# The order of the query tiles in a sparse attention stage, turned round in both halves

## Chip, cores and metric

The kernel runs on one core of one Trainium2 chip. The metric is the device time of one execution in microseconds (us). Three runs of the kernel before gave 2013.47, 2013.79 and 2018.54 us, with a median of 2013.79 us.

## What is computed

Two transformer parts run one after the other on a sequence of 512 tokens of width 1024, in float32. The first is a layer with windowed attention, a gated convolution and a mixture of experts. The second has two layers: one with index-selected and forgetting attention and an MLP, and one with the sparse attention that this document is about, and an MLP. The sparse attention adds three branches for each of 16 heads in two groups of keys (g = 0 and 1), cut here to what matters:

```python
p_c = masked_softmax(s_c, cmp_end[None, :] <= t[:, None])      # 31 compressed keys
o_c = einsum('bghqn,bngd->bqghd', p_c, vc)
valid_s = tok_pos <= t                                          # selected blocks, causal
o_s = einsum('bghqk,bgqkd->bqghd', masked_softmax(s_s, valid_s), v_g)
valid_w = (pos >= 0) & (pos <= t) & (pos > t - WINDOW_2)        # window of 512, causal
o_w = einsum('bghqk,bkgd->bqghd', masked_softmax(s_w, valid_w), vw)
out = gb[..., 0:1] * o_c + gb[..., 1:2] * o_s + gb[..., 2:3] * o_w
```

With 512 tokens all 8 blocks are kept and the window reaches over the whole sequence, so both long branches are plain causal attention: the queries of tile t (128 tokens, t = 0 to 3) need (t + 1) x 128 keys. Tile 3 has four times the columns of tile 0.

## The kernel before

Each engine runs its own hand-written list of work, and the lists are tied by semaphores. TensorE (PE) does the products and the transposes, VectorE (DVE) and ScalarE (ACT) work on the results in PSUM and split operands into a high and a low float32r part, GpSimd (POOL) scales probabilities and makes low parts of weights, and SyncE (SP) issues the loads of weights into a ring of three slots.

The sparse attention is a software pipeline over 136 **items**, built once as the list `nsa` (L745 to L753). There are two halves (c = 0, 1: four of a group's eight heads each), in each half four query tiles t, and in each tile 17 items: 16 "pair" items (4 heads x 2 branches x 2 groups, each with n = (t + 1) x 128 key columns), and one "cmp" item for the compressed branch, always 256 columns wide. Every engine loops over the steps i and handles item i, or an item some steps back:

- PE, step i (L2119): the scores of item i into a PSUM bank (L2142, two matmuls of n columns; L2138 for cmp), the n/128 transposes of the probabilities of item i - 7 (L2153), and, where item i - 10 closes a group of four, the values of the four (L2112, 4 x n/128 x 2 instructions' worth of work, shown as 8, 16, 24 or 32 rows; L2102 for cmp). Scores of an item wait until the item that had its bank before is masked. Up to item 15 there are two banks (psS), afterwards four (psS, psA).
- DVE: masks item i and takes its minimum for the softmax (L3619), takes reciprocals (L3579), and copies the transposed probabilities of odd items from PSUM (L3603).
- ACT: the exponential of item i (L2181, `scr<-scr,stat`), and the copies of the even items' transposed probabilities (`big<-psT`). A closed tile's output is rounded by ACT (`nsa_out_hi`), and DVE makes its low part (`nsa_out_lo`).
- POOL: multiplies by reciprocal and gate (L1322; L1318 for cmp).

Other work is put between the items at fixed step numbers, which do not depend on the tile. At steps 3, 4, 12 and 13 PE makes the scores of the compressed keys (L2089), and at steps 5, 6, 7 and 9 it turns the queries of the second half (L1346). Both use the two psA banks in turn, so each waits for the one two before it to be copied out. ACT copies the queries one step later (two copies for each turn, `nsa_q<-psA`) and DVE takes their low part two steps later (two instructions):

```python
NSA_JOBS = (("cmp", 0), ("cmp", 1), ("query", 4), ("query", 5), ("query", 6), ("query", 7), ("cmp", 2), ("cmp", 3))
NSA_STEPS = (3, 4, 5, 6, 7, 9, 12, 13)
```

At items 82, 86, 90 and 94 (`PRESPLIT`) ACT and POOL split a quarter each of the first weights of the output projection (`no_part`, L1290 on POOL). When the scores of item 67 are done, SP issues the load of `no1` into the slot where the queries of the first half lay. After the last item the pipeline drains, and the output projection (L1482, `no_part`, `nsa_out_hi`, `nsa_out_lo`) waits for the output of all eight tiles. Each tile's values gather in one of two psO banks, by `bank`.

Of the kernel before, what the change touches and what calls it, by code (L numbers as in the profile page):

```python
# [13 lines left out]
P = 128  # L14
T = 512
NT = T // P
# [318 lines left out]
def build(nc, w, out):  # L335
    ctx = ExitStack()
    with ctx:
# [300 lines left out]
        for g in range(2):  # L638
            for t in range(NT):
                lo, hi = max(0, t - 1), min(NT - 1, t + 1)  # L640
                n = (hi - lo + 1) * P
# [26 lines left out]
        for kind in ("fox", "latent"):  # L668
            for hp in range(4):
                for t in range(NT):  # L670
                    for half in range(2):
                        pairs.append(dict(fox=kind == "fox", hp=hp, half=half, t=t, n=(t + 1) * P,
                                          bank=hp + 4 * (kind == "latent"), chunk=hp + 4 * (kind == "fox"),
# [70 lines left out]

        nsa = []  # L745
        for c in range(2):
            for t in range(NT):
                for j in range(4):
                    for branch in range(2):
                        for g in range(2):  # L750
                            nsa.append(dict(kind="pair", c=c, t=t, j=j, branch=branch, g=g, n=(t + 1) * P,
                                            head=8 * g + 4 * c + j, bank=NT * c + t, first=not j, closes=bool(branch and g)))
                nsa.append(dict(kind="cmp", c=c, t=t, g=1, n=2 * P, bank=NT * c + t, index=NT * c + t, closes=True))  # L753
        n_nsa = len(nsa)
        last_of = {it["bank"]: i for i, it in enumerate(nsa)}
        n_items = n_band + n_pairs
# [2908 lines left out]
```

How the kernel before makes its waits and increments, by code:

```python
        def product(eng, n, i=0):  # L934
            eng.wait_ge(proj_ready, i * 10 + (n + 1))
# [1 line left out]
        def copied(eng, n, i=0):  # L938
            eng.wait_ge(proj_evacuated[n % 2], i * 5 + (n // 2 + 1))
# [33 lines left out]
        def consumed(eng, l, i):  # L974
            kind, e, n = MLP_PIECES[i]
            if kind == "up":
                product(eng, job(f"mlp{l}", MLP_FIRST[kind, e] + n))
            elif e < LAST and n in KEPT:
                eng.wait_ge(down_product, len(KEPT) * (LAST * l + e) + KEPT.index(n) + 1)
            elif e < LAST:
                product(eng, job(f"mlp{l}", MLP_FIRST[kind, e] + 2 * SHARED.index(n) + 1))
            else:
                product(eng, job(f"mlp{l}", MLP_FIRST[kind, e] + NT * (n // 2 + 1) - 1))
# [64 lines left out]
        def spilled(eng):  # L1049
            eng.wait_ge(slots_ready, 2)
            return eng.value_load(spill_expert[0:1, 0:1], min_val=0, max_val=SPILL)
# [23 lines left out]
            def experts():  # L1077
# [1 line left out]
                def gate_up(n):  # L1079
                    if n >= UNITS:
                        sp.wait_ge(gu_ready, (n - UNITS) // 2 + 1)
                    e = PAIRS * (n % 2) + n // 2
                    load_gate_up(n % UNITS, slice(e, e + 1), gu_arrived[n % UNITS])
# [5 lines left out]
                    load_down(n % UNITS, slice(e, e + 1), dn_arrived[n % UNITS])  # L1089
                sp.wait_ge(y_zeroed, 16)
                sp.wait_ge(*held[gu_slot[0]])
# [1 line left out]
                product(sp, JOBS["mergea"] + KD - 1)  # L1094
                down(0)
                sp.wait_ge(*held[gu_slot[1]])
                gate_up(1)
```

## Time and profile before

| what | value |
|---|---|
| median of three runs | 2013.79 us |
| the profiled execution's own time | 2014.52 us |
| its span, first to last instruction | 2012.7 us |
| mean granted TensorE clock | 0.982 |
| busy over the span: PE, DVE, ACT, POOL | 94%, 50%, 41%, 28% |
| sparse attention: first scores | 1444.1 us |
| first instruction of the output projection | 1617.7 us |

The span is 1.8 us shorter than the profiled execution's own time, and that time is 0.7 us above the median. Times inside the span are counted from its first instruction. A PE instruction's duration includes its way through the array, so instructions that follow each other overlap, and "busy" overstates the work; the step from one start to the next is the better price.

### The profile page before, as it was taken

The page shows a single profiled execution, that of the slowest core. Times are in us where ns is not written, and L with a number is a line of the kernel's source. Part 1 is how long each engine was busy: PE and PEld are TensorE (multiplying, and loading weights), DVE is VectorE, ACT ScalarE, POOL GpSimd, SP SyncE. Part 2 cuts the span into 40 slices and gives each one's busy share as a digit, 9 for nine tenths or more (in the row PEclk, how much of TensorE's full clock was granted, in tenths as well). Part 3 has the DMA queues.
Part 4 walks back from the last instruction along what each step waited for, and adds up shares of the span by engine and source line. Part 5 has one row for each costly group of instructions (what it writes and reads, how often), then busy time and mean ns, then how long its engine had stood idle before and what let it go on. Part 6 is the DMA issues. An engine that isn't in the chain of part 4 may idle for free.

```text
span 2012.7 us, 28214 instructions
## 1 busy us (share of the span) xinstructions
PE 1883.7 (94%) x11022; PEld 1471.7 (73%) x11022; DVE 1012.7 (50%) x2027; ACT 815.8 (41%) x1507; POOL 559.2 (28%) x396
## 2 busy tenths in 40 slices
PE   7999999898888999988999999999899999999997
PEld 6878889832323893457888888888867798888886
DVE  2170442521113625863366676822566715676677
ACT  5123551311112413364554544343367626544542
POOL 2244331011110420154421123233146533113111
PEclk9999999999899999999999999999999999999999
DMA  6223303799999320201123223311103012223321
GB/s 234 85 84 123 129 1 147 274 375 419 421 420 346 133 103 0 84 1 43 43 97 113 84 84 126 136 57 43 42 2 85 2 43 84 84 84 126 126 84 42
DMA packets 86149, 252.10 MB, mean 125 GB/s; under 512 B 12132, under 2 KB 19492, under 8 KB 73728
## 3 DMA queue, kind: packets, MB, share of 16 engines
q1 hardware_dynamic: 80624, 237.83, 32.0%
q0 software_dynamic: 4592, 9.30, 1.3%
q10 hardware_dynamic: 800, 3.15, 0.4%
q8 instruction: 89, 1.46, 0.3%
q14 instruction: 44, 0.36, 0.1%
HBM read 241.89 MB, written 15.73 MB: 128 GB/s over the span
## 4 chain that ended last, share of the span: by engine, by line
PE 48%; DVE 4%; issue 2%; ACT 2%; POOL 0%; DVEq 0%; ACTq 0%
PE psA L1482 33%; PE psO L1647 2%; PE psT L1647 2%; PE psS L1647 2%; PE psO L2112 2%; PE psT L2153 1%; DVE x L2711 1%; PE psA L1598 1%; PE psS L2142 1%; PE psO L1546 1%; PE psT L1578 1%; ACT big L2181 1%; PE psA L2142 1%; DVE scr L3619 1%; PE psA L2022 1%
## 5 line engine op out<-in xcount | busy, mean ns | idle before, releaser
L1187 POOL TENSOR_TENSOR w_slot<-ring,w_slot 128x1024 fp32r<-128x1024 f32 (+2 forms) x80 | 208.4, 2620 | 550.8 <-ACT w_slot L2181 550.3
L1482 PE MATMUL psA<-hT_hi,w_slot 128*128 128x512 f32 x960 | 297.9, 389 | 0.0
L2181 ACT ACTIVATE w_slot<-ring 128x1024 fp32r<-128x1024 f32 (+2 forms) x178 | 191.9, 1088 | 176.9 <-PE psA L1482 76.9
L1482 PEld LDWEIGHTS psA<-hT_hi,w_slot 128*128 128x128 f32 x960 | 180.2, 188 | 37.5
L2711 DVE TENSOR_TENSOR x<-psA,x 128x512 f32<-128x512 f32 (+1 forms) x206 | 122.4, 623 | 147.1 <-PE psA L1482 142.5
L1482 PE MATMUL psA<-hT_lo,w_slot 128*128 128x512 f32 x480 | 186.7, 389 | 0.0
L2711 DVE TENSOR_TENSOR w_slot<-ring,w_slot 128x1024 fp32r<-128x1024 f32 x98 | 119.8, 1224 | 115.8 <-ACT w_slot L2181 115.8
L2181 ACT ACTIVATE big<-psA 128x512 f32<-128x512 f32 (+7 forms) x145 | 63.9, 465 | 255.5 <-PE psA L1482 140.1
L1482 PE MATMUL psA<-w_slot,hid_part 128*128 128x512 f32 x672 | 161.4, 389 | 0.0
L2181 ACT ACTIVATE scr<-scr,stat 128x384 f32<-128x384 f32 (+3 forms) x224 | 124.4, 556 | 68.0 <-DVE stat L3619 37.9
L1482 PEld LDWEIGHTS psA<-w_slot,hid_part 128*128 128x128 f32 x672 | 126.2, 188 | 26.1
L1187 POOL TENSOR_TENSOR ring_lo<-ring,early_hi 128x1024 fp32r<-128x1024 f32 x34 | 82.5, 2430 | 128.0 <-ACT early_hi L2181 128.0
L1322 POOL TENSOR_SCALAR scr<-scr,stat,big 128x128 f32<-128x128 f32 (+3 forms) x128 | 77.4, 616 | 108.5 <-DVE stat L3579 108.0
L1482 PEld LDWEIGHTS psA<-hT_lo,w_slot 128*128 128x128 f32 x480 | 90.1, 188 | 18.4
L2711 DVE TENSOR_TENSOR hid_part<-scr,hid_part 128x512 fp32r<-128x512 f32 x98 | 98.9, 1032 | 3.0 <-ACT hid_part L2181 1.8
L2181 ACT ACTIVATE hid_part<-scr 128x512 fp32r<-128x512 f32 x98 | 59.7, 625 | 98.3 <-DVE scr L2711 98.3
L1482 PE MATMUL psA<-w_slot,hT_hi 128*128 128x256 f32 (+2 forms) x512 | 93.9, 287 | 5.3 <-DVE tok L2715 2.7
L2711 DVE TENSOR_TENSOR big<-psA,small 128x512 f32<-128x512 f32 x32 | 20.6, 685 | 140.1 <-PE psA L1346 140.1
L1482 PE MATMUL psA<-hT_lo_early,early_hi 128*128 128x512 f32 x224 | 88.0, 393 | 0.0
L1840 PE MATMUL psS<-ring,big 128*64 128x512 f32 x192 | 74.9, 671 | 12.7 <-issue 12.7
L1482 PEld LDWEIGHTS psA<-w_slot,hT_hi 128*128 128x128 f32 x512 | 81.4, 197 | 5.9 <-issue 3.0
L2181 ACT ACTIVATE big<-psS 128x256 f32<-128x256 f32 (+1 forms) x20 | 7.3, 365 | 190.6 <-PE psS L1840 162.7
(440 smaller groups left out, 4473.5 us busy)
## 6 DMA issues: line engine op xcount, KB each, us to landing
ring<-in_mlp_w SPq DMA_DIRECT2D x32, 2048.0 KB, 8.1
ring<-in_w_in SPq DMA_DIRECT2D x8, 2048.0 KB, 8.0
ring<-in_w_gate_e SPq DMA_DIRECT2D x14, 1024.0 KB, 17.9
ring<-in_w_up_e SPq DMA_DIRECT2D x14, 1024.0 KB, 22.8
ring<-in_w_down_e SPq DMA_DIRECT2D x13, 1024.0 KB, 27.1
big<-in_w_down_e SPq DMA_DIRECT2D x12, 1024.0 KB, 28.2
ring<-in_ab_w_in SPq DMA_DIRECT2D x5, 2048.0 KB, 8.3
scr<-in_w_down_e SPq DMA_DIRECT2D x7, 1024.0 KB, 25.3
```

The source lines that it names most:

```text
L1187: nc.gpsimd.tensor_tensor(part(w_lo, c), raw_piece(c), part(w_hi, c).bitcast(F32), ALU.subtract)\
L1322: nc.gpsimd.tensor_scalar(at, at, fac[:, n_items + i:n_items + i + 1], gate3[:, it["t"], it["head"], 1 + it["branch"]:2 + it["branch"]], A ...
L1482: ins = pe.matmul(o, a, b, start=(at == 1), stop=(at == 3 * len(terms)))
L1546: ins = pe.matmul(o[HD * half:HD * (half + 1), t * P:(t + 1) * P], v[:, b, 2 * it["hp"] + half, :], pt[half][:, b * P:(b + 1) * P], start= ...
L1578: ins = pe.transpose(psT[k % 2][:, b * P:(b + 1) * P], pair_probs[k % PROBS][:, b * P:(b + 1) * P], ident)
L1598: ins = pe.matmul(out[f][:, some], a[:, k, 0:P], b[:, k, some], start=(k == 0 and a is wh and b is hT_hi), stop=(k == KD - 1 and a is wl))
L1647: ins = pe.matmul(KEPT_BANK[q][t][:, :], a[:, k, at], b[:, k, :], start=(not e and k == 0 and a is hi and b is wh), stop=(e == LAST - 1 an ...
L1840: ins = pe.matmul(psS[p][at:at + ROWS, :].rearrange("p (h n) -> p h n", h=2), xT[:, p, k, at:at + ROWS], gu[(2 * b + half) % UNITS][:, k], ...
L2112: ins = pe.matmul(o[HD * g:HD * (g + 1), at:at + P], v2[:, b, branch, g, 0:HD], pt[g][:, b * P:(b + 1) * P], start=(it["first"] and not br ...
L2142: ins = pe.matmul(o[:, 0:it["n"]], query(4 * it["c"] + it["j"], it["g"])[:, it["t"] * P:(it["t"] + 1) * P], nsa_k[:, it["branch"], it["g"] ...
L2181: return nc.scalar.activation(o, i, f, **kw)
L2711: return nc.vector.tensor_tensor(o, a, b, op)
```

## The change

The tiles of each half are taken in the order 3, 2, 1, 0, where they were taken 0, 1, 2, 3. `place` now numbers the PSUM bank, so that banks follow each other as before, while `t` still names the tile. Nothing is added or removed, and the fixed step numbers of the other work stay.

```diff
         for c in range(2):
-            for t in range(NT):
+            for place, t in enumerate((3, 2, 1, 0)):
                 for j in range(4):
                     for branch in range(2):
                         for g in range(2):
                             nsa.append(dict(kind="pair", c=c, t=t, j=j, branch=branch, g=g, n=(t + 1) * P,
-                                            head=8 * g + 4 * c + j, bank=NT * c + t, first=not j, closes=bool(branch and g)))
-                nsa.append(dict(kind="cmp", c=c, t=t, g=1, n=2 * P, bank=NT * c + t, index=NT * c + t, closes=True))
+                                            head=8 * g + 4 * c + j, bank=NT * c + place, first=not j, closes=bool(branch and g)))
+                nsa.append(dict(kind="cmp", c=c, t=t, g=1, n=2 * P, bank=NT * c + place, index=NT * c + t, closes=True))
```

On PE, at the start of the stage (`psS` holds scores, `psT` turned probabilities, `nsa_q_90` the queries of the first half, `par` and `const` constants and parameters), before:

```order
L2142 MATMUL psS<-nsa_k,nsa_q_90 128x128 x6
L2089 MATMUL psA<-nsa_q_90,big 32x512 x4
L2142 MATMUL psS<-nsa_k,nsa_q_90 128x128 x2
L2089 MATMUL psA<-nsa_q_90,big 32x512 x4
L2142 MATMUL psS<-nsa_k,nsa_q_90 128x128 x2
L1346 MATMUL psA<-const,tok 128x128 x4
L2142 MATMUL psS<-nsa_k,nsa_q_90 128x128 x2
L1346 MATMUL psA<-const,tok 128x128 x4
```

and now:

```order
L2142 MATMUL psS<-nsa_k,nsa_q_90 128x512 x6
L2089 MATMUL psA<-nsa_q_90,big 32x512 x4
L2142 MATMUL psS<-nsa_k,nsa_q_90 128x512 x2
L2089 MATMUL psA<-nsa_q_90,big 32x512 x4
L2142 MATMUL psS<-nsa_k,nsa_q_90 128x512 x2
L1346 MATMUL psA<-const,tok 128x128 x4
L2142 MATMUL psS<-nsa_k,nsa_q_90 128x512 x2
L1346 MATMUL psA<-const,tok 128x128 x4
```

The fixed work keeps its places, and the scores between its pieces are four times as wide.

On PE, the last rows of the stage, from the last scores (L2138) to the first row of the output projection, before:

```order
L2138 MATMUL psA<-const,big 128x128 x2
L2153 MATMUL psT<-const,scr 128x128 x8
L2112 MATMUL psO<-big 64x128 x16
L2153 MATMUL psT<-const,scr 128x128 x16
L2112 MATMUL psO<-big 64x128 x16
L2153 MATMUL psT<-const,scr 128x128 x6
L2112 MATMUL psO<-big 64x128 x16
L2102 MATMUL psO<-big 64x128 x8
L1482 MATMUL psA<-no_part_72,nsa_out_hi_93 128x256
```

and now:

```order
L2138 MATMUL psA<-const,big 128x128 x2
L2153 MATMUL psT<-const,scr 128x128 x2
L2112 MATMUL psO<-big 64x128 x4
L2153 MATMUL psT<-const,scr 128x128 x4
L2112 MATMUL psO<-big 64x128 x4
L2153 MATMUL psT<-const,scr 128x128 x3
L2112 MATMUL psO<-big 64x128 x4
L2102 MATMUL psO<-big 64x128 x8
L1482 MATMUL psA<-no_part_72,nsa_out_hi_93 128x256
```

What is left to do after the last scores shrinks to a quarter in the transposes and values of pair items and stays in those of the cmp item. (One row of this kind stands as two instructions in the trace, for float32.)

## Rows read from the trace of the kernel before

**Rows 1.** Busy time by stretch: each tile's scores, then the drain; header first.

```profile
core 0: us, PE busy (x) PEld busy (x) DVE busy (x) ACT busy (x) POOL busy (x), PEclk, DMA share, GB/s
1444.00:1470.60 26.60, 17.84 (x112) 10.53 (x100) 13.31 (x59) 14.63 (x50) 5.28 (x12) 0.74 0.00 1
1470.60:1484.60 14.00, 13.05 (x117) 10.37 (x118) 10.84 (x52) 10.75 (x39) 8.40 (x17) 1.00 0.01 2
1484.60:1503.30 18.70, 17.81 (x168) 14.83 (x167) 14.15 (x56) 13.24 (x42) 9.90 (x17) 1.00 0.01 1
1503.30:1527.80 24.50, 23.08 (x215) 18.39 (x214) 17.64 (x57) 17.17 (x45) 13.88 (x19) 1.00 0.01 1
1527.80:1545.20 17.40, 16.82 (x194) 14.56 (x192) 11.16 (x57) 10.86 (x42) 8.09 (x16) 1.00 0.92 242
1545.20:1561.40 16.20, 13.20 (x119) 10.42 (x119) 11.78 (x58) 13.60 (x49) 14.09 (x22) 1.00 0.01 3
1561.40:1580.10 18.70, 17.81 (x168) 14.77 (x167) 14.15 (x56) 13.04 (x42) 10.18 (x17) 1.00 0.01 2
1580.10:1604.00 23.90, 22.51 (x210) 17.82 (x209) 17.28 (x56) 16.60 (x44) 13.32 (x19) 1.00 0.00 1
1604.00:1617.70 13.70, 11.00 (x146) 9.43 (x144) 7.14 (x18) 6.11 (x13) 4.28 (x6) 1.00 0.01 2
```

**Rows 2.** Chain that ended last, by time: start us, us taken, what.

```profile
1446.08 1.07 PE psA L2089 x8
...
1471.22 0.59 PE psO L2112 x8
...
1595.47 1.02 PE psO L2102 x16
...
1597.15 0.44 PE psT L2153 x4
1597.59 0.46 PE psA L2142 x2
...
1600.30 1.90 PE psO L2112 x32
```

**Rows 3.** Timeline of PE, first stretch: start, us, instruction, [idle before <-releaser].

```profile
1453.24 1.12 PE L1346 MATMUL psA<-const,tok 128*128 128x128 f32 x4 [2.13 <-DVE nsa_q L2711]
...
1458.17 1.12 PE L1346 MATMUL psA<-const,tok 128*128 128x128 f32 x4 [2.70 <-DVE nsa_q L2711]
...
1464.67 1.55 PE L2089 MATMUL psA<-nsa_q,big 128*32 128x512 f32 x8
```

**Rows 4.** Groups by form, ACT, 1444 to 1618 us: count, busy us, mean ns, idle before.

```profile
L2181 ACT ACTIVATE scr<-scr,stat 128x512 f32<-128x512 f32 x32 | 22.9, 718 | 15.6 <-DVE stat L3619 15.4
...
L2181 ACT ACTIVATE big<-psT 128x512 f32<-128x512 f32 x16 | 9.4, 588 | 4.6 <-PE psT L2153 4.6
...
L2181 ACT ACTIVATE nsa_q<-psA 64x512 fp32r<-64x512 f32 x8 | 4.7, 586 | 0.1
```

**Rows 5.** Groups by form, DVE, the same stretch.

```profile
L3603 DVE COPY big<-psT 128x512 f32<-128x512 f32 x16 | 10.9, 683 | 9.7 <-PE psT L2153 9.5
...
L3619 DVE CUSTOM_DVE_ANT_0 scr<-psS,const 128x512 f32<-128x512 f32 x16 | 10.9, 679 | 0.0
...
L2711 DVE TENSOR_TENSOR nsa_q<-psA,nsa_q 64x512 fp32r<-64x512 f32 x8 | 5.5, 688 | 2.3 <-ACT nsa_q L2181 2.2
```

**Rows 6.** Busy time, part of the first stretch (PEclk is the column after POOL).

```profile
1451.00:1465.00 14.00, 8.46 (x39) 5.53 (x42) 7.85 (x23) 7.04 (x21) 1.97 (x5) 0.54 0.00 0
```

**Rows 7.** Groups by form, the weight splits inside the stage, ACT and POOL.

```profile
L2181 ACT ACTIVATE no_part<-ring 128x512 fp32r<-128x512 f32 x4 | 2.5, 614 | 0.0
...
L1290 POOL TENSOR_TENSOR no_part<-ring,no_part 128x512 fp32r<-128x512 f32 x4 | 5.3, 1328 | 0.0
```

**Rows 8.** Timeline of the drain, all engines: last scores, last output, projection.

```profile
1604.03 0.38 PE L2138 MATMUL psA<-const,big 128*128 128x128 f32 x2
...
1616.32 0.60 ACT L2181 ACTIVATE nsa_out_hi<-psO 128x512 fp32r<-128x512 f32 x1 [2.94 <-PE psO L2102]
...
1617.74 0.48 PE L1482 MATMUL psA<-no_part,nsa_out_hi 128*128 128x256 f32 x2 [1.47 <-ACT nsa_out_hi L2181]
```

**Rows 9.** Timeline of SP's queue: the load of the last projection slot.

```profile
1527.67 1.27 SPq L1170 DMA_DIRECT2D ring<-in_c_w_out  x2
```

## The prediction

> **What bounds the kernel now.** I read the busy time cut at the first scores of each tile first, because the change moves whole tiles and nothing else [rows 1]. The nine stretches are eight tiles and the drain, 173.7 us together. PE has granted clock 1.00 in eight of them and 0.74 in the first. Then I took from the chain of waits what PE's pieces cost when they follow each other [rows 2]: scores of a tile-3 item 0.46 us, its four transposes 0.44 us, so 0.11 or so per 128 columns for either; values of a group of four 1.90 us for tile 3 (32 instructions) and 0.59 for tile 0 (8), so about 1.46 and 1.02 for tiles 2 and 1 (24 and 16); values of the cmp item 1.02; one product with the compressed keys 1.07.
>
> With these prices I add up PE's work in each stretch. A stretch holds the scores of its own 17 items, but the transposes of items 7 back and the values of items 10 back, so it depends on the tile ahead of it too: of that one, 6 pair items and the cmp item are transposed and 3 groups and the cmp item get their values. Written as "tile after tile", with length, work and what is unfilled (the difference):
>
> - tile 0, first: 26.6, work 10.0 (6.0 of it the fixed work: 4 products and 4 query turns of 0.44), unfilled 16.6
> - 1 after 0: 14.0, 11.0, unfilled 3.0
> - 2 after 1: 18.7, 16.1, unfilled 2.6
> - 3 after 2: 24.5, 21.5, unfilled 3.0
> - 0 after 3: 17.4, 13.6, unfilled 3.8
> - 1 after 0, with the weight splits: 16.2, 11.0, unfilled 5.2
> - 2 after 1: 18.7, 16.1, unfilled 2.6; 3 after 2: 23.9, 21.5, unfilled 2.4
> - drain of tile 3: 13.7, 9.6, unfilled 4.1
>
> Work is 130.4 and unfilled time 43.3 us. So the stage is PE's with small losses everywhere but at its start, and the start is where a tile of little PE work meets fixed work that waits for ACT and DVE. PE stands 2.13 us and 2.70 us there for DVE's low parts of the queries [rows 3], and during it the granted clock is 0.54, near the lower level of 1.2 GHz [rows 6].
>
> **The change, part by part.** PE's work is the same in sum: by the same prices it comes out as 19.9 (tile 3 first), 20.2, 14.9, 9.6 (tiles 2, 1, 0), 17.6 (3 after 0), 20.2, 14.9, 9.6 and a drain of 3.7, 130.6 in all. Only the unfilled time can move.
>
> *First stretch.* I follow the waits with tile-3 durations: mask 0.68 (the next can start after 0.60), exponential 0.72 (next after 0.70), copies from psT 0.59 on ACT and 0.68 on DVE, two query copies 1.2 on ACT and two low parts 1.4 on DVE [rows 4, 5].
> (1) Start to the first query wait's end: the first two masks and DVE's small copies between them take ACT's second exponential to 3.2 us after the start; then ACT does three exponentials (2.1), the two copies of products with an exponential between (1.9), waits about 0.4 for mask 5, and does one exponential more (0.7) and the query copies (1.2), and DVE its low parts (1.4): about 11 us. Before it was 9.2, from 1444.0 to 1453.24 [rows 1, 3].
> (2) To the second query wait's end: query turn 0.44, scores 0.46, transposes with their latency 0.6, ACT copy 0.6, exponential 0.7, query copies 1.2, low parts 1.4: 5.4 us, before 4.9.
> (3) To the last product with the compressed keys: turn and scores 0.9, transposes and scores 0.9, transposes 0.6, DVE copy and mask 1.4, exponential 0.7, query copies 1.2, low parts 1.4: 7.1 us, before 6.5, at the low clock [rows 3].
> (4) To the first scores of the next tile: product 1.07, a wait for a mask 0.3, three steps of 0.9, values 1.9, the cmp step 0.7: 6.7 us, before 5.9.
> Together 30.2 us for 19.9 of work: 10.3 unfilled, a gain of 6.3 against 16.6. Its bounds: all waits overlapping with PE's work except the two query waits (7 unfilled) and all waits as now (16.6).
>
> *The seven tile changes.* Before, five of them without splits or tile 3 ahead left 2.4 to 3.0 unfilled, 2.7 on average, tile 0 after 3 left 3.8, and the splits added 2.2 to their stretch [rows 1]. I take 2.7 for each and 1.2 for the splits: these now fall on the last items of tile 3 and on tile 2, where ACT has more slack under PE (four splits are 2.5 us of ACT and 5.3 of POOL [rows 7]). That is 20.1 against 22.6, a gain of 2.5. Bounds: 2.4 each and no cost of splits (16.8), or 3.8 each and 2.2 (28.8).
>
> *The drain.* The cmp item's own latency (masks, exponential, POOL, transposes, copy, values, rounding) doesn't shrink with the tile, and the last output still goes over ACT and DVE before the projection, 1.4 us [rows 8]. PE's work falls from 9.6 to 3.7, but less of the latency lies under it: 4.6 unfilled against 4.1, a loss of 0.5. Bounds 4.1 and 5.5.
>
> *What hides the rest.* The load of `no1` starts when half of the scores are done, 83.6 us into the stage [rows 9]; by the lengths above that is now 83 us, and the slot is wanted only in the second half of the projection. No wait is added, and no queue is passed: SP and POOL keep their lists.
>
> Sum: 6.3 + 2.5 - 0.5 = 8.3. I take off 0.8 because PE still stands twice for some 3 us in the first stretch, and the clock may fall for a short while there. Gain 7.5 against the profiled execution's own 2014.5 us: 2007.0. That execution is 0.7 above the median of the runs, so against the median it is 2006.3 us.
>
> **A rule that speaks against it.** In the fourth stretch, where a third of PE's work is transposes (6.6 of 21.5 us), the granted clock is 1.00 throughout [rows 1]. The Trainium skill ("TensorE: Matmul & The Clock Gate", "PE-mode transpose") says that a transpose does not count as activity for the clock as a matmul does. Here the trace does not bear that out as a danger in a dense stretch, but the first stretch is not dense; what a low clock there would cost is the third rival.
>
> **The rivals.**
> - *The start only swaps its waits* (0.26). ACT and DVE carry the same 10 us of query copies among exponentials and masks 0.3 to 0.4 us longer each, 17 of either. If PE also waits for masks in between, through the two psS banks, the first stretch is 34 us instead of 30.2. For it: each engine runs strictly in order and [rows 3] show the waits in series. Against it: DVE is busy only 13.3 of 26.6 us there. Gain 3.5: 2010.3 us.
> - *The later stretches fill better too* (0.15). Bursts of values run ahead of narrower tiles, and everything after a wide tile finds its probabilities ready: unfilled 2.4 each and no cost of splits, gain 11: 2003 us. Against it is tile 0 after 3, with 3.8.
> - *The clock stays low from the first query wait on* (0.07, ends slower). In the first stretch PE would pay a further 10 us for the pieces on the path in (2) to (4), and if the low clock goes on into tile 2, up to 20 more. It decides from the point where 13.5 us of PE's path run at 1.2 GHz: 7.5 to gain and 6 to be slower by 0.3%. For it: 14 us of the first stretch ran so before [rows 6]. Against it: tile 3 gives PE twice the work there. Price 15: 2021 us.
> - That the change does not do what it says is left out: the two places shown in the order of the instructions say that it does.
>
> By the rule of the skill the clock would be at its lower level in the first stretch, and the time that of the third rival or a little below it.
>
> **How the numbers follow.** The forecast has 0.52. 0.3% of the median is 6.0 us, about what a measurement of this kernel can tell from no change. The forecast's own range, a gain of 5 to 10 us, lies mostly over that: 0.44 of it faster, 0.08 the same. The second rival is all faster (0.15), the first nearly all the same (0.25, 0.01 faster), the third 0.05 slower and 0.02 the same. That makes 0.60, 0.35 and 0.05. For 8 in 10 the range must hold the forecast, the first rival and most of the second, 2002.5 to 2012.5; the bounds together (3 us slower to 15 faster) are wider than that, and leave out what would need all terms at one end.
>
> **What would show it.** First scores of the second tile 30 us after the stage's first, against 26.5, with two waits for `nsa_q` of some 3 us left; clock 1.00 or nearly in that stretch; 12 to 13 us for the stretches of tile 0 and 20 to 21 for tile 3 after 0; 8 us between last scores and projection, against 13.7; everything outside the stage unchanged. It is wrong if the first stretch is over 33 us, if a clock of 0.5 shows for more than a few us, or if tile changes leave over 3.5 us each.

## The result, and the profile after

The changed kernel took 2022.12 us, median of ten runs (2019.91 to 2023.85); the kernel before took 2014.26 us beside it (2013.13 to 2018.54). The ratio is 1.0037, with a 95% interval of 1.0029 to 1.0045. The forecast was 2006.3 us in a range up to 2012.5, so the change costs 8 us where it should have given 8. The profiled execution took 2023.29 us, 1.2 above the median.

Busy time by stretch, the changed kernel, with the columns of [rows 1]: tiles 3, 2, 1, 0 of the first half, the same of the second, and the drain.

```profile
1443.90:1482.00 38.10, 25.86 (x163) 16.31 (x154) 21.76 (x59) 21.09 (x49) 9.14 (x12) 0.91 0.00 1
1482.00:1506.50 24.50, 23.36 (x225) 20.13 (x226) 14.32 (x51) 13.77 (x39) 11.29 (x17) 0.93 0.01 2
1506.50:1524.00 17.50, 17.01 (x182) 14.29 (x180) 12.68 (x57) 12.21 (x43) 9.19 (x16) 1.00 0.01 1
1524.00:1538.80 14.80, 13.12 (x133) 10.59 (x131) 10.28 (x57) 10.31 (x45) 8.51 (x18) 1.00 0.00 1
1538.80:1559.20 20.40, 19.49 (x155) 14.43 (x155) 15.68 (x56) 14.39 (x42) 10.67 (x17) 1.00 0.83 208
1559.20:1584.80 25.60, 22.12 (x227) 18.58 (x226) 16.34 (x57) 17.63 (x49) 17.44 (x22) 1.00 0.01 2
1584.80:1602.30 17.50, 16.99 (x182) 14.28 (x180) 12.69 (x57) 12.19 (x43) 9.53 (x17) 1.00 0.01 1
1602.30:1616.60 14.30, 12.71 (x130) 10.40 (x129) 9.78 (x53) 9.80 (x42) 8.31 (x17) 1.00 0.01 2
1616.60:1625.00 8.40, 5.26 (x53) 3.32 (x51) 4.83 (x21) 4.28 (x16) 3.25 (x7) 1.00 0.01 2
```

The stage takes 181.1 us, against 173.7 [rows 1]. With the prediction's PE work for each stretch, the unfilled times are 18.2, 4.3, 2.6, 5.2, 2.8, 5.4, 2.6, 4.7 and 4.7, together 50.5 against 43.3 before. The first stretch alone is 38.1 where 30.2 was forecast. So that stretch holds half of the 15.8 us between forecast and result. Its granted clock is 0.91, against 0.74 before, so on the whole it was less slowed by the clock than the stretch before the change; but the prediction had priced (2) to (4) at full clock and taken off only 0.8, and what the low clock cost is worked out below.

Busy time after the stage, to the end of the program, the changed kernel and then the kernel before:

```profile
1625.00:2021.50 396.50, 382.61 (x1916) 325.91 (x1916) 246.95 (x308) 180.22 (x239) 104.28 (x41) 0.99 0.24 85
```

```profile
1617.70:2012.70 395.00, 381.14 (x1916) 324.56 (x1916) 246.75 (x308) 180.23 (x239) 104.26 (x41) 0.99 0.24 86
```

Same work, 1.5 us more. It lies where the projection ends and the first products of the MLP begin; in the changed kernel that piece has granted clock 0.91, before 1.00:

```profile
1672.00:1690.00 18.00, 14.74 (x106) 13.62 (x105) 8.12 (x15) 8.75 (x14) 7.74 (x4) 0.91 0.12 41
```

```profile
1664.70:1682.70 18.00, 14.75 (x118) 13.62 (x118) 8.11 (x15) 8.91 (x16) 7.77 (x4) 1.00 0.14 40
```

The stage's 7.4 us and these 1.5 are, but for rounding, the 8.8 us between the two spans.

PE's timeline at the end of the first stretch of the changed kernel (it answers to [rows 3]):

```profile
1455.67 1.11 PE L1346 MATMUL psA<-const,tok 128*128 128x128 f32 x4 [2.55 <-DVE nsa_q L2711]
...
1459.00 0.60 PE L2153 MATMUL psT<-const,scr 128*128 128x128 f32 x4
1462.61 1.12 PE L1346 MATMUL psA<-const,tok 128*128 128x128 f32 x4 [3.02 <-DVE nsa_q L2711]
...
1465.89 0.60 PE L2153 MATMUL psT<-const,scr 128*128 128x128 f32 x4
...
1471.45 1.07 PE L2089 MATMUL psA<-nsa_q,big 128*32 128x512 f32 x8 [0.19 <-DVE nsa_q L2711]
1472.82 0.73 PE L2142 MATMUL psS<-nsa_k,nsa_q 128*128 128x512 f32 x2 [0.30 <-DVE stat L3619]
1473.38 0.60 PE L2153 MATMUL psT<-const,scr 128*128 128x128 f32 x4
1473.91 1.97 PE L2112 MATMUL psO<-big 128*64 128x128 f32 x32
1475.81 0.73 PE L2142 MATMUL psS<-nsa_k,nsa_q 128*128 128x512 f32 x2
1476.38 0.60 PE L2153 MATMUL psT<-const,scr 128*128 128x128 f32 x4
1478.36 0.73 PE L2142 MATMUL psS<-nsa_k,nsa_q 128*128 128x512 f32 x2 [1.39 <-DVE stat L3619]
...
1479.79 0.41 PE L2138 MATMUL psS<-const,big 128*128 128x128 f32 x2 [0.25 <-ACT big L2181]
...
1482.02 0.61 PE L2142 MATMUL psS<-nsa_k,nsa_q 128*128 128x384 f32 x2 [1.39 <-DVE stat L3619]
```

and DVE's over the same time:

```profile
1472.76 0.67 DVE L3619 CUSTOM_DVE_ANT_0 scr<-psS,const 128x512 f32<-128x512 f32 x1
...
1477.01 0.69 DVE L3603 COPY big<-psT 128x512 f32<-128x512 f32 x1 [3.58 <-PE psT L2153]
1477.62 0.68 DVE L3619 CUSTOM_DVE_ANT_0 scr<-psS,const 128x512 f32<-128x512 f32 x1
```

The two views have to be laid over each other. The scores of item 13 start at 1472.82, and with 0.73 us for their two instructions they are done by 1473.6. DVE has been idle since 1473.4, but it doesn't mask them: its list has a copy of item 7's transposes ahead of mask 13. PE makes those transposes one step later (1476.38), behind item 14's scores, and both stand behind 1.9 us of values. So DVE idles 3.58 us, mask 13 runs at 1477.62, and only then may PE write item 15's scores into the bank: 1478.36, after 1.39 us of waiting. **PE and DVE wait for each other in a ring.** PE turns item i - 7 at step i, but DVE (odd items) and ACT (even items) copy item i - 6 at step i, *before* the mask or exponential of item i. In each of the prediction's steps (2) to (4) this ring lies across the path, and the copy, the mask and the values in it are 0.69, 0.68 and 1.9 us for tile 3, where tile 0 had 0.29, 0.28 and 0.59.

### The profile page after: what moved, and what is told of

The parts are those of the page before. It is cut to its first block, busy times and chain, and to the rows that moved or that the text cites. A ratio compares the mean times of both kernels' runs of the same rounds, so it can differ in the third digit from the quotient of the medians.

```text
span 2021.5 us, 28214 instructions
## 1 busy us (share of the span) xinstructions
PE 1888.1 (93%) x11022; PEld 1474.4 (73%) x11022; DVE 1014.1 (50%) x2027; ACT 815.6 (40%) x1507; POOL 559.3 (28%) x396
## 4 chain that ended last, share of the span: by engine, by line
PE 48%; DVE 4%; issue 2%; ACT 2%; POOL 0%; DVEq 0%; ACTq 0%
PE psA L1482 33%; PE psO L1647 2%; PE psT L1647 2%; PE psS L1647 2%; PE psO L2112 2%; PE psT L2153 2%; DVE x L2711 1%; PE psA L1598 1%; PE psS L2142 1%; PE psO L1546 1%; PE psT L1578 1%; DVE scr L3619 1%; PE psA L2142 1%; PE psA L2022 1%; ACT big L2181 0%
## 5 line engine op out<-in xcount | busy, mean ns | idle before, releaser
L1322 POOL TENSOR_SCALAR scr<-scr,stat,big 128x512 f32<-128x512 f32 (+3 forms) x128 | 77.5, 616 | 119.8 <-DVE stat L3579 119.7
L1482 PEld LDWEIGHTS psA<-hT_lo,w_slot 128*128 128x128 f32 x480 | 90.1, 188 | 18.7
## 6 DMA issues: line engine op xcount, KB each, us to landing
ring<-in_w_up_e SPq DMA_DIRECT2D x14, 1024.0 KB, 20.3
```

What stands on the lines that cost most here:

```text
L1322: nc.gpsimd.tensor_scalar(at, at, fac[:, n_items + i:n_items + i + 1], gate3[:, it["t"], it["head"], 1 + it["branch"]:2 + it["branch"]], A ...
L1482: ins = pe.matmul(o, a, b, start=(at == 1), stop=(at == 3 * len(terms)))
```

## The experiments

Each run was timed in five rounds; ratios are to the kernel before on the same chip. Lengths of stretches are from first scores to first scores, in each profiled execution.

### Which resource holds the start: banks or query copies

Two simple theories came first. Theory A: the first 16 items have only two psS banks, and scores wait for masks through them. Theory B: the four query turns, close together at steps 5, 6, 7 and 9, pile up copies on ACT and DVE. What theory A blames is undone by a third bank, in both kernels:

```diff
-            return psS[i % 2] if i < MORE_BANKS else (psS + psA)[i % 4]
+            return (psS[1], psO[1], psS[0])[i % 3] if i < MORE_BANKS else (psS + psA)[i % 4]
```

> The changed order with a third PSUM bank for the scores of items 0 to 15 (one psO bank, which is idle until item 30's step). Theory A (two score banks are too few for tile 3: a score waits for the mask of two items before, which waits behind DVE's copy of a transposed item, five waits, 5.1 us in all): first stretch 38.1 us falls to 33 to 34, time 2017 to 2018 us. Rival B (the fixed work is a series chain over ACT and DVE of 5.9 us of waits for query low parts, and a third bank only lets PE arrive there earlier): first stretch 37 to 38.5, time 2021 to 2023.

Measured: 2025.53 us, ratio 1.0054 (1.0040 to 1.0067). The first stretch stays 38.1 us, and the second takes 25.3, 0.8 more than in the changed kernel. Where PE waited in the first, for the changed kernel:

```profile
PE psA L1346 <- DVE nsa_q L2711: 5.6, 2, 3.0
PE psS L2142 <- DVE stat L3619: 5.1, 5, 1.5
```

and with the third bank (us in all, times, longest):

```profile
PE psA L1346 <- DVE nsa_q L2711: 5.6, 2, 3.0
PE psA L2089 <- DVE nsa_q L2711: 2.0, 1, 2.0
PE psS L2138 <- ACT big L2181: 1.9, 1, 1.9
PE psS L2142 <- DVE stat L3619: 1.4, 1, 1.4
```

3.7 us of waits for masks are gone, and 3.4 us come back as waits for DVE's low parts and ACT's copies. Theory A, which expected 33 to 34 us for this stretch, falls: the banks are where the wait shows, not what makes it.

> The kernel before, with the same third bank. Theory A: with tile 0 a mask takes 0.28 us instead of 0.69 and a copy 0.29 instead of 0.69, so the bank binds less than half as much: 1 to 2.5 us faster than before, 2012 to 2013 us. Rival B: no difference over 0.5 us, 2014.

Measured on the kernel before: 2016.27 us, ratio 1.0006 (0.9997 to 1.0015), first stretch 26.8. No difference in the time that can be told from zero, as rival B had it. In its profiled execution the waits for masks fell from 2.4 to 0.6 us, but the second stretch took 15.3 us instead of 14.0, with a second piece at the lower clock (1471.1 to 1474.5 us).

Theory B was tried by spreading the fixed steps:

```diff
-NSA_STEPS = (3, 4, 5, 6, 7, 9, 12, 13)
+NSA_STEPS = (1, 2, 3, 4, 7, 8, 12, 13)
```

> The changed order with the fixed work spread: steps 1, 2, 3, 4, 7, 8, 12, 13 in place of 3, 4, 5, 6, 7, 9, 12, 13, so that a query turn stands four steps behind the one whose bank it takes, not two. Theory B (the first stretch is a series chain: turn, ACT copies, DVE low parts, next turn, with tile 3's masks, exponentials and copies between its links): the waits of 2.55 and 3.02 us before the query turns go, first stretch 38.1 to 32 to 34, time 2016 to 2018 us. Rival (the sum of the work of ACT and DVE per step is the limit, wherever the links stand): 37 to 38 and 2021 to 2023.

Measured: 2023.55 us, ratio 1.0038 (1.0026 to 1.0050), first stretch 37.7. PE's waits there:

```profile
PE psS L2142 <- DVE stat L3619: 7.6, 6, 2.7
PE psA L1346 <- DVE nsa_q L2711: 1.4, 2, 1.0
```

The query waits shrink from 5.6 to 1.4 us, the mask waits grow from 5.1 to 7.6, and PE stands 1.8 us before a product with the compressed keys for a reason that the profile doesn't name. What was gained on one link was lost on others: theory B, which expected 32 to 34 us, falls as well, in its simple form.

> The kernel before with the same spread steps. Theory B: the waits of 2.13 and 2.70 us go, and with them the low clock; first stretch 26.5 to 22 to 23, time 2010 to 2011 us, 3 to 4 us under the kernel before. Rival: 26 and 2014.

Measured on the kernel before: 2016.54 us, ratio 1.0006 (0.9997 to 1.0015), first stretch 26.7. The low clock did not go, as theory B had hoped: PE ran at it from 1455.5 to 1465.7 us and again from 1469.1 to 1475.9, and the second stretch took 15.5 us instead of 14.0.

### Which half, which place

```diff
-            for place, t in enumerate((3, 2, 1, 0)):
+            for place, t in enumerate(((0, 3, 2, 1), (3, 2, 1, 0))[c]):
```

> Tiles 0, 3, 2, 1 in the first half and 3, 2, 1, 0 in the second: only the first tile is put back beside the fixed work. Theory that the whole loss is the first stretch (38.1 against 26.5 us, less than the 9.9 us of more PE work there explains): first stretch 26.5 again, and the time 2014 to 2016 us. Rival (descending order loses in each stretch that follows a wider tile, and at tile 0): 2018 to 2020 us.

Measured: 2020.75 us, ratio 1.0029 (1.0016 to 1.0041). With tile 0 first the first stretch is 26.6 us again, and tile 3 after 0 takes 19.7, tile 2 22.2, tile 1 19.2 (with the work that a tile 3 leaves behind it), and the second half is 21.8, 25.6, 17.4, 14.3 and a drain of 9.8: 176.6 us in all, 2.9 above the kernel before. So 4.5 of the stage's 7.4 us hang on the wide tile at the start, and the rest doesn't. Two stretches of this one run have the same PE work, tile 2 after tile 3, without and with the weight splits:

```profile
1491.60:1513.80 22.20, 21.60 (x229) 18.75 (x227) 15.82 (x57) 14.56 (x42) 10.26 (x16) 1.00 0.01 2
1554.80:1580.40 25.60, 22.11 (x227) 18.57 (x226) 16.33 (x57) 17.64 (x49) 17.46 (x22) 1.00 0.01 2
```

The splits cost 3.4 us in this place; the prediction had 1.2. In the changed kernel's stretch with splits PE and its weight loads waited so, and in the stretch without (of this run) the second of the two waits was 0.9 us, once:

```profile
PE psT L2153 <- ACT big L2181: 3.5, 3, 1.3
...
PEld psT L2153 <- POOL scr L1322: 4.6, 4, 1.6
```

A split of 1.27 us on POOL stands in its list between scalings of 0.66 us, and one of 0.61 us on ACT ahead of the copies of transposes. Both kinds of wait grow beside them; which of the two engines sets the 3.4 us was not tried apart.

```diff
+            for place, t in enumerate(((0, 1, 2, 3), (3, 2, 1, 0))[c]):
```

> First half as before (0, 1, 2, 3), second half turned round (3, 2, 1, 0). By unfilled PE time: start 16.6, then 3.0, 2.6, 3.0 as before, then tile 3 after 3 about 2, tile 2 with the splits 5.4, tile 1 2.5, tile 0 4.8 and the drain 4.6 as in the changed kernel: 44.5 against 43.3, so 1 us slower than before, 2014 to 2016.5 us. If turning round the second half alone were a gain (its stretches with the drain are 86.2 us in the changed kernel and 89.9 before), 2010 to 2011 us.

Measured: 2018.63 us, ratio 1.0020 (1.0011 to 1.0029). Stretches 26.6, 14.0, 18.7, 49.8 (the two tiles 3 side by side), 25.6, 17.4, 14.3 and a drain of 9.4: 175.8 us, 2.1 above the kernel before. The order turned in the second half alone loses too.

```diff
+            for place, t in enumerate(((3, 2, 1, 0), (0, 1, 2, 3))[c]):
```

> Only the first half turned round (3, 2, 1, 0), the second as before. The unfilled times of the changed kernel's first half (18.2, 4.3, 2.5, 5.2), about 4 for tile 0 after tile 0, and those of the kernel before for the rest (5.2, 2.6, 2.4, 4.1) make 48.5 against 43.3: 2019.5 us. If the loss were all in the second half, 2014 us.

Measured: 2021.78 us, ratio 1.0026 (1.0014 to 1.0037). Stretches 38.1, 24.5, 17.4, 26.8 (two tiles 0), 16.2, 18.7, 23.9 and a drain of 13.7: 179.4 us. So the new order of the first half alone makes 5.7 of the stage's 7.4 us of loss.

### The lag between the lists

Theory S: what makes tile 3 dear at the start is the ring, PE's transposes of item i - 7 against copies of item i - 6 on the other engines. Theory L: it is the plain latency of mask, exponential and scaling, and a shorter lag makes PE wait for that. The two are told apart by taking PE's turns and values one item earlier (6 and 9 back), in the three lists of the stage:

```diff
-AHEAD, MORE_BANKS, PRESPLIT = 2, 16, (82, 86, 90, 94)
+AHEAD, NSA_AHEAD, MORE_BANKS, PRESPLIT = 2, 1, 16, (82, 86, 90, 94)
...
-                    k = i - TURN_LAG - AHEAD
+                    k = i - TURN_LAG - NSA_AHEAD
...
-                    k = i - VALUE_LAG - AHEAD
+                    k = i - VALUE_LAG - NSA_AHEAD
```

> The changed order, with transposes and values one step earlier in PE's list (items 6 and 9 back instead of 7 and 10). Theory L (what is unfilled at tile 0 and 1 behind wider tiles is the latency from scores over mask, exponential, reciprocal and POOL to the transpose, which must fit into 7 steps of PE): with 6 steps every stretch of tile 0 and 1 gets 1 to 3 us longer, time 2027 to 2032. Theory S (DVE's copy of item i - 6 waits in front of mask i for the transposes that PE makes one step later, 41 us of waits in all, and that delays everything): the waits of DVE L3603 halve, time 2015 to 2019.

Measured: 2015.60 us, ratio 1.0003 (0.9994 to 1.0012). Stretches 32.9, 22.4, 17.9, 13.6, 24.0, 23.6, 17.9, 12.6 and a drain of 7.7: 172.7 us where the changed kernel takes 181.1. DVE's waits for transposes over the whole stage, changed kernel, then this one:

```profile
DVE big L3603 <- PE psT L2153: 52.2, 36, 4.3
```

```profile
DVE big L3603 <- PE psT L2153: 37.5, 33, 2.7
```

They fall by 28%, not by the half that was expected, and the longest from 4.3 to 2.7 us. The time lies where theory S had it (2015 to 2019), and L, with 2027 or more, falls.

> The kernel before with the shorter lag (6 and 9) everywhere. Theory S with the loop's price by width: copy and mask are 0.57 us with tile 0 and 1.38 with tile 3, so the first stretch gains 1 to 2 us of 26.5, the others together 0 to 3: 2010.5 to 2013.5 us, and the order 0 to 3 stays ahead of 3 to 0 (2015.6 with the same lag). Rival (with the shorter lag the order no longer matters, or the turned order profits alone): 2014.5 to 2016.

The same edit on the kernel before: 2013.64 us, ratio 0.9995 (0.9986 to 1.0004), stage 172.5 us. The lag is worth 8.4 us of the stage with the wide tiles first and 1.2 with the narrow first, and with lag 6 the two orders take the same (172.7 and 172.5). So the stage's loss hangs on the two together: the wide-first order loses only with the long lag. The 8.4 us are not all waits, though. With lag 6 the wide-first kernel has none of its three pieces at the lower clock left, while the narrow-first one keeps its long one (13.6 us, 13.7 before).

Is it the start alone? Only PE's items up to step 16 take the short lag, step 17 turns nothing, and everything behind is as in the changed kernel:

```diff
-                    k = i - TURN_LAG - AHEAD
+                    k = i - TURN_LAG - 1 if i < MORE_BANKS + 1 else i - TURN_LAG - AHEAD if i > MORE_BANKS + 1 else -1
...
-                    k = i - VALUE_LAG - AHEAD
+                    k = i - VALUE_LAG - 1 if i < MORE_BANKS + 1 else i - VALUE_LAG - AHEAD if i > MORE_BANKS + 1 else -1
```

> The changed order with the shorter lag (6 and 9) for PE's steps 0 to 16 only, and 7 and 10 from step 18 on. If the loop of DVE's copy, mask and PE's next step is what made the first stretch 38.1 us and not 30.2, this takes it to 33 as the shorter lag everywhere did (32.9), and leaves the other stretches as in the changed kernel: 2016.5 to 2018. If the gain of the shorter lag was spread or came from the granted clock by luck, 2020 to 2022.

Measured: 2016.12 us, ratio 1.0005 (0.9996 to 1.0014). Its first two stretches:

```profile
1444.00:1476.90 32.90, 25.03 (x197) 15.94 (x190) 22.93 (x61) 22.61 (x53) 10.76 (x14) 1.00 0.00 1
1476.90:1497.30 20.40, 19.27 (x192) 16.56 (x191) 13.14 (x47) 12.09 (x36) 9.62 (x16) 1.00 0.01 2
```

Together they take 53.3 us, where the changed kernel takes 62.6 for the same work (one group of values and four transposes, 2.3 us, lie in the first stretch here and in the second there). The prediction had 53.1 for the two. DVE's waits for transposes from 1438 to 1483 us, in this kernel, then in the changed one:

```profile
DVE big L3603 <- PE psT L2153: 6.1, 4, 2.0
```

```profile
DVE big L3603 <- PE psT L2153: 11.1, 4, 4.0
```

The second row is the waits for items 1, 3, 7 and 9 (4.02, 1.81, 3.58 and 1.69 us). With the short lag these are 1.64, 0, 1.88 and 0.59, together 4.1 instead of 11.1; the fourth wait of the first row, 2.0 us, is for item 11, later than anything in the second. PE's wait before item 15's scores is 0.48 us instead of 1.39:

```profile
1472.56 0.73 PE L2142 MATMUL psS<-nsa_k,nsa_q 128*128 128x512 f32 x2 [0.48 <-DVE stat L3619]
```

**About half of these 9.3 us is the clock.** Behind each of its two long query waits the changed kernel's PE does a turn, scores, transposes and scores again before the transposes on which DVE's copy waits. From 1455.67 to 1459.00 and from 1462.61 to 1465.89 that takes 3.33 and 3.28 us at the lower clock. With the short lag the same four pieces run at full clock and take 1.86 us both times:

```profile
1455.73 0.66 PE L1346 MATMUL psA<-const,tok 128*128 128x128 f32 x4 [2.11 <-DVE nsa_q L2711]
...
1457.59 0.60 PE L2153 MATMUL psT<-const,scr 128*128 128x128 f32 x4
1460.29 0.66 PE L1346 MATMUL psA<-const,tok 128*128 128x128 f32 x4 [2.11 <-DVE nsa_q L2711]
...
1462.15 0.60 PE L2153 MATMUL psT<-const,scr 128*128 128x128 f32 x4
```

That is 2.9 us in the first stretch. In the second, the changed kernel has a third such piece; from the 4.00 us that PE is busy there at granted clock 0.57 (shown below) it costs an estimated 1.7 us, and the same work took 2.3 us less in the run that starts with tile 0. The other 4 to 5 us are waits at full clock, those for items 7 and 9 and behind them. So the ring costs by its waits, and as much again by the clock that falls behind them; that the ring's waits are what makes it fall is argued from the three versions with a wide tile first and the short lag in whose start it doesn't fall (a fourth, with the query work spread, has one piece of 3.4 us), and is not shown apart.

> The changed order with the shorter lag everywhere and the spread steps 1, 2, 3, 4, 7, 8, 12, 13. With the loop loosened, what is left of the query waits (2.12 and 2.11 us) can go now: first stretch 32.9 to 29 or 30, time 2012 to 2013 us. If the work of ACT and DVE per step is the limit, as without the shorter lag (38.1 to 37.7): 32 to 33, 2015 to 2016.

Lag 6 in the whole stage with the spread steps of above: 2019.79 us, ratio 1.0025 (1.0016 to 1.0034), where 2012 to 2016 was expected. The first stretch is 35.2 us, 2.3 more than without the spread, with 3.4 us at the lower clock that the version without it doesn't have. Query work at earlier steps made no version faster; why it costs here was not followed up.

### The parts that help, put together

Tile 3 first in the first half, the original order in the second (its drain is longer, but the splits cost 2.2 us there [rows 1] and 3.4 in the turned order), and the short lag of PE at the start, so the edit of the first half alone and the one above:

```diff
+            for place, t in enumerate(((3, 2, 1, 0), (0, 1, 2, 3))[c]):
...
+                    k = i - TURN_LAG - 1 if i < MORE_BANKS + 1 else i - TURN_LAG - AHEAD if i > MORE_BANKS + 1 else -1
...
+                    k = i - VALUE_LAG - 1 if i < MORE_BANKS + 1 else i - VALUE_LAG - AHEAD if i > MORE_BANKS + 1 else -1
```

> First half turned round with the shorter lag for PE's steps 0 to 16 as in e9, second half 0 to 3 as in the kernel before. If the stretches add up as measured (32.9, 20.4 and 17.4 from e9, 26.8 for the two tiles 0 from e8, 16.2, 18.7, 24.0 and 13.6 from the kernel before: 170.0 against 173.7 us), it is 3 to 4 us faster than the kernel before: 2010.5 to 2011.5. If each of the turned order's stretches only moves its loss to the next, 2014 to 2016.

Measured: 2010.63 us, ratio 0.9977 (0.9968 to 0.9986), faster than both kernels by 4.5 and about 11.5 us. The stage takes 170.1 us (32.9, 20.4, 17.4, 26.8, 16.2, 18.7, 24.0, drain 13.7), with 170.0 expected from the parts, with granted clock 1.00 in the whole of it, and the rest of the program 395.0 as before:

```profile
1443.40:1613.50 170.10, 150.03 (x1432) 118.53 (x1425) 118.04 (x458) 115.26 (x359) 87.26 (x140) 1.00 0.10 26
```

One comparison is missing: the short lag at the start alone, on the kernel before. With the short lag in its whole stage its first two stretches took 39.7 us instead of 40.6, so an estimated 0.9 of the 3.6 us that the stage gains could have been had without turning anything.

## Why the prediction was wrong

**The failed step is the walk through the first stretch, (2) to (4), with its allowance for the clock.** Step (1) held: 11.7 us for 11. Step (2) took 6.9 for 5.4, (3) 8.8 for 7.1 and (4) 10.6 for 6.7, together 38.1 (with rounding) for 30.2. Two things were wrong in it.

- *The wait.* The walk followed one path at a time and never asked what stands ahead of a mask in DVE's list. It counted "a wait for a mask 0.3" in (4), where there are 0.30, 1.39 and 1.39. The missing link is the copy of an earlier item ahead of each mask and exponential, which PE feeds one step late. In (4) the clock is 1.00, so its 3.9 us of miss are all waits and what hangs on them. With the lag of PE shortened at the start alone, (4) took 7.9.
- *The clock.* The forecast took off 0.8 us for it. The low clock costs 1.5 us in (2), 1.4 in (3) and about 2 in the next stretch. In (2) and (3) that is nearly the whole miss of 1.5 and 1.7. The ring is in them too, for with the short lag they took 4.6 and, without the group of values that comes earlier then, 6.8 us, less than was forecast: the walk had other terms of them too long.

With the short lag at the start the first two stretches took 53.3 us together, and the forecast had 53.1. That they agree is in part luck, as the single steps don't.

**The gain was sized as if it didn't depend on the tile's width.** The bound of 16.6 unfilled ("all waits as now") was no bound: the waits in the ring hold copies, masks and values of the tile itself, and unfilled time came out at 18.2.

**The first rival** (PE also waits for masks in between, 34 us) was the nearest in mechanism. It was too short by 4 us, and the third bank shows that its reason, the two banks, was not the cause. The ring was in no case of mine.

**The seven tile changes** were forecast at 20.1 unfilled and came out at 27.6. Three terms of it failed:
- Tile 0 after 1: 2.7 forecast, 5.2 and 4.7 measured. Weight loads of transposes wait 2.0 us for POOL there in the changed kernel, where before, in tile 0 after 3, they waited 0.5:

```profile
PEld psT L2153 <- POOL scr L1322: 2.0, 4, 0.7
```

```profile
PEld psT L2153 <- POOL scr L1322: 0.5, 1, 0.5
```

Before, wide values of tile 3 (1.9 us) ran ahead of tile 0 and covered the latency of mask, exponential, reciprocal and scaling; after tile 1 there is less to cover it. With lag 6 these stretches were 13.6 and 12.6 us, but they also hold less work then, so this reading rests on the rows and was not tried apart.

- The splits: 1.2 forecast, 3.4 measured by two stretches of equal work. "ACT has more slack under PE" was read from busy shares, and they don't show where a split stands in a list: PE waited 3.5 us there for ACT's copies, and its weight loads 4.6 us for POOL's scalings.
- Tile 2 after 3 in the first half: 24.5 us, where the same work took 22.2 in another run. From 1482.5 on PE ran at the lower clock for some 3.4 us, after its wait of 1.39 us:

```profile
1482.50:1486.50 4.00, 4.00 (x37) 3.51 (x35) 0.74 (x2) 1.22 (x4) 1.42 (x2) 0.57 0.00 0
```

**What held.** The work was conserved, and the stretches whose neighbours are wide came out as forecast: 17.5 for 17.6 twice, 20.4 for 20.3. The drain took 8.4 us for 8.3. Two waits for `nsa_q` of some 3 us stayed (2.55 and 3.02). The second half with its drain is shorter, 86.2 us against 89.9, but that is no gain: by the prediction's prices it holds 66.0 us of PE's work now and held 71.8 before, since the tail of the first half that it takes over is tile 0's and no longer tile 3's. Its unfilled time rose from 18.1 to 20.2. The load of `no1` went under the work as before: the stretch it falls into, with DMA share 0.83, took its forecast 20.4.

**The third rival**, a clock that stays low, did not come as it stood: there were three falls of 3.4 us each (from 1455.4, 1462.2 and 1482.7), against one of 13.7 us before. But the clock did cost some 5 us of the stage where it had 15, so a third of its price was real. That it had the change slower was right in part for another reason. The Trainium skill ("TensorE: Matmul & The Clock Gate", "PE-mode transpose") says that a transpose doesn't count as activity for the clock as a matmul does. The fourth stretch before [rows 1] and every stretch here from the third on have 1.00 with transposes in all of them, and the first stretch, for which the prediction drew the lower level from that rule, has 0.91. No run has a stretch of transposes alone, so none shows whether they count for less.

The sum of the misses: first stretch 7.9, tile 0 twice 4.5, tile 2 with the splits 1.5 and without 1.6 make 15.5, and rounding in the other stretches 0.2. Less the 0.8 that the forecast had taken off for the clock, and with 1.5 outside the stage, that is 16.4, and the forecast of 2006.3 becomes 2022.7. The profiled execution lies 1.2 us above its median where the one before lay 0.7 above its own, which leaves 2022.2; 2022.12 was measured.

The 1.5 us outside, which the prediction had at nothing, go with the clock. In the profiled executions the rest of the program took 395.0 us in the three versions with no low clock around the end of the projection (the kernel before, the same with the third bank, and the last one), 396.3 to 396.5 in the six with 3.4 us of it there, and 397.5 to 397.7 in the four with 6.8. The one with the turned second half alone has 396.3, with the low clock at the projection's start instead. What sets these falls off stays open.

## What to carry to other kernels

In a pipeline of hand-written lists, write for each step of each engine which item it takes from the others and *where in their lists* that item's work stands; a copy that asks for the next step's transposes, put ahead of this step's mask, closes a ring. Here it cost little with narrow tiles first and much with wide ones. Before turning an order, add up unfilled time by stretch and ask of each piece of it whether it is fixed or scales with the tile that now stands there. If one order looks bound by its start, try the lag and the order together: here turning either half or both lost, the short lag in the whole stage gained nothing that can be measured in either order, and the two, each where it helps, gave 4.5 us.

## What was not expected of the hardware

The clock can fall behind short waits, and what it costs comes on top of the wait. The changed kernel has granted clock 0.57 over 1455 to 1459 us and 0.53 over 1462 to 1465.5, each behind a wait of 2.6 or 3.0 us among short bursts, and 0.57 over 1482.5 to 1486.5 behind 1.39 us; that last one comes with 2.3 us more for the same work than in the run where the clock stayed at 1.00. With PE's lag one item shorter all three are gone (1.00 in both stretches), though PE still waits 2.11 us twice there; in the kernel before, the clock fell at a wait of 2.13 us. So the length of one wait doesn't decide it.

```profile
1455.00:1459.00 4.00, 3.33 (x13) 2.84 (x14) 0.61 (x1) 0.47 (x1) 0.00 (x0) 0.57 0.00 0
1462.00:1465.50 3.50, 2.89 (x11) 2.59 (x12) 2.63 (x5) 1.14 (x3) 0.76 (x2) 0.53 0.00 0
```

A short drain can cost again in the stage after it. With the second half alone turned round, PE did little in the drain of tile 0, and its clock was low from there into the start of the projection; the rest of the program took 1.3 us more than in the kernel before:

```profile
1616.00:1623.00 7.00, 5.54 (x38) 4.99 (x39) 1.12 (x2) 2.51 (x3) 1.51 (x1) 0.53 0.01 2
```

In the changed kernel's own drain the clock stayed at 1.00, so it differs from one version to the next, and nothing found here forecasts it.
